# A two-layer conv, latent-attention and expert step on one core: expert matrices with eight rows per partition, and a reordered further round

## The reference, cut to what matters

```python
for e in range(N_EXPERTS):                       # 16
    h = jax.nn.silu(t @ w1[e]) * (t @ w3[e])     # w1, w3: 1024 x 512
    out = out + gates[:, e:e + 1] * (h @ w2[e])  # w2: 512 x 1024
```

## Time and profile before

| what | us |
|---|---|
| median of 3 runs | 1077.71 |
| lowest, highest of them | 1077.51, 1089.82 |
| profiled execution, its own time | 1089.26 |
| span of its trace | 1087.6 |
| layer 0's experts, on PE (from about 207 to 476) | 269 |
| layer 1's experts, on PE (from about 794 to 1071) | 277 |

### The profile page before, as it was taken

One profiled execution on the slowest core, in us unless ns is written; L12 is line 12 of the kernel. 1 busy time (PEld: TensorE's weight loads), 2 busy tenths in 40 slices (PEclk: granted clock), 3 DMA queues, 4 the chain that ended last, 5 costly groups with the idle time before them and its releaser, 6 DMA issues.

```text
span 1087.6 us, 14379 instructions
## 1 busy us (share of the span) xinstructions
PE 964.6 (89%) x4814; PEld 480.5 (44%) x4815; DVE 339.5 (31%) x815; ACT 168.6 (16%) x335; POOL 105.5 (10%) x198
## 2 busy tenths in 40 slices
PE   6979989899989989979989888889798999888993
PEld 4646535443333333336646644454543333332331
DVE  0935464522122221251234432304522122211125
ACT  1000042111111110012123232220111111011100
POOL 0260000101000000013000033000110000000000
PEclk9989999799999999989998899989698999999997
DMA  7974454999979999977213101566386499999981
GB/s 188 253 242 126 126 195 154 345 370 329 379 264 362 377 375 385 395 243 251 59 35 101 64 20 53 199 222 262 127 286 239 169 370 376 378 383 378 383 306 49
DMA packets 131654, 266.96 MB, mean 245 GB/s; under 512 B 7480, under 2 KB 39252, under 8 KB 131585
## 3 DMA queue, kind: packets, MB, share of 16 engines
q1 hardware_dynamic: 121200, 237.74, 61.9%
q10 hardware_dynamic: 5009, 16.15, 4.2%
q0 software_dynamic: 5392, 12.34, 4.1%
HBM read 259.78 MB, written 7.15 MB: 245 GB/s over the span
## 4 chain that ended last, share of the span: by engine, by line
PE 71%; DMA 8%; DVE 8%; SPq 8%; ACT 4%; issue 2%; DVEq 0%; ACTq 0%
PE bank L1009 16%; PE bank L1017 9%; DMA w<-in_e_w 5%; PE wide L1052 4%; PE bank L902 4%; SPq L420 4%; PE bank L791 3%; PE bank L956 3%; DMA dbuf<-in_a_w_pw 3%; SPq L423 3%; PE wide L902 3%; PE wide L791 2%; PE wide L1809 2%; PE bank L807 2%; PE bank L1787 2%
## 5 line engine op out<-in xcount | busy, mean ns | idle before, releaser
L1009 PE MATMUL bank<-w,dbuf 128*64 128x512 f32 x960 | 216.5, 604 | 16.3 <-DMA w<-in_e_w 14.6
L1009 PEld LDWEIGHTS bank<-w,dbuf 128*64 128x64 f32 x960 | 74.2, 139 | 153.9 <-issue 153.6
L1017 PE MATMUL bank<-w,dbuf 128*64 128x512 f32 x480 | 122.6, 657 | 10.9 <-DVE dbuf L1455 10.9
L1460 DVE COPY dbuf<-bank 64x512 f32<-64x512 f32 x64 | 44.1, 689 | 166.3 <-PE bank L1017 165.8
L1451 DVE TENSOR_TENSOR dbuf<-dbuf,bank 64x512 f32<-64x512 f32 x32 | 22.1, 690 | 201.6 <-ACT dbuf L709 201.6
L709 ACT ACTIVATE dbuf<-bank 64x512 f32<-64x512 f32 x32 | 18.9, 592 | 412.8 <-PE bank L1009 412.8
L1017 PEld LDWEIGHTS bank<-w,dbuf 128*64 128x64 f32 x480 | 40.4, 149 | 77.7 <-issue 77.7
L1052 PE MATMUL wide<-dbuf,ukT 128*128 128x512 f32 x128 | 62.9, 617 | 3.0 <-DVE dbuf L1460 3.0
L549 POOL COPY idx_col<-idx 64x1 int32 (+1 forms) x32 | 5.8, 180 | 560.8 <-PE bank L956 375.8
L956 PEld LDWEIGHTS bank<-ident,dbuf 64*128 64x128 f32 x448 | 38.9, 160 | 41.4 <-issue 36.8
L536 POOL DMA_DIRECT2D w<-in_cache_kpe x64 | 34.4, 538 | 217.3 <-PE bank L1787 116.7
(11 more groups left out here) (365 smaller groups left out, 1148.1 us busy)
## 6 DMA issues: line engine op xcount, KB each, us to landing
w<-in_e_w SPq DMA_DIRECT2D x90, 2048.0 KB
dbuf<-in_a_w_pw SPq DMA_DIRECT2D x16, 512.0 KB, 7.3
w<-u_rows SPq DMA_DIRECT2D x32, 142.0 KB, 3.0
dbuf<-in_a_w_pw ACTq DMA_DIRECT2D x1, 4096.0 KB, 17.1
dbuf<-in_e_w SPq DMA_DIRECT2D x2, 2048.0 KB, 14.9
w<-in_cache_ckv SPq DMA_DIRECT2D x32, 128.0 KB, 2.8
dbuf<-in_cache_ckv SPq DMA_DIRECT2D x32, 128.0 KB, 2.1
dbuf<-in_b_w_o SPq DMA_DIRECT2D x2, 2048.0 KB, 8.6
```

Source lines behind the costliest of these rows:

```text
L1009: last = nc.tensor.matmul(bank[n * C:(n + 1) * C], x[:, k], w[n][k], start=(k == 0), stop=(k == KD - 1))
L1017: last = nc.tensor.matmul(bank[n * C:(n + 1) * C], h[:, k], w[k][:, n * 512:(n + 1) * 512], start=(k == 0), stop=(k == 3))
L1460: last = V.tensor_copy(y_pair[s * C:(s + 1) * C, h * 512:(h + 1) * 512], DOWN[h * C:(h + 1) * C, :])
```

## The change

Four edits. The rows of the first and third matrices are split as "(p k)", so a partition gets rows 8p to 8p + 7, 16 KB that adjoin in DRAM and in SBUF. Channel 8p + k then has to be at partition p of block k of the turned tokens, so `turn_rows` (for gathered rows) and `turn_more` read every eighth element of the gathered row; the hidden rows turn as before. In the further round PE waits for `y_copied` only ahead of the down product, and turns `hot_more` behind a new semaphore `m_built`, ahead of the hidden rows; `up_more` takes the eight blocks in another order in each quarter. The semaphore `own_ready` is gone, `own` counts on `ld_att`.

```diff
-                src = a[("e_w1", "e_w3")[n]][l].rearrange("e (k p) f -> p e k f", p=P)[:, bass.ds(e, 1)]
+                src = a[("e_w1", "e_w3")[n]][l].rearrange("e (p k) f -> p e k f", p=P)[:, bass.ds(e, 1)]
...
-            def turn_rows(bank, src, n, r0=0):
+            def turn_rows(bank, src, n, r0=0, strided=True):
+                cols = src.rearrange("c (p k) -> c k p", k=n) if strided else src.rearrange("c (k p) -> c k p", k=n)
                 for k in range(n):
-                    last = nc.tensor.matmul(bank[:, k * C:(k + 1) * C], src[:, k * P:(k + 1) * P],
+                    last = nc.tensor.matmul(bank[:, k * C:(k + 1) * C], cols[:, k],
                                             ident[r0:r0 + C, r0:r0 + C], start=True, stop=True, is_transpose=k > 0)
...
             def turn_more():
+                cols = xg_more.rearrange("c (p k) -> c k p", k=KD)
                 for k in range(KD):
-                    last = nc.tensor.matmul(TURN[:, k * H:(k + 1) * H], xg_more[:, k * P:(k + 1) * P], ident[0:H, 0:H],
+                    last = nc.tensor.matmul(TURN[:, k * H:(k + 1) * H], cols[:, k], ident[0:H, 0:H],
...
             def up_more(w):
-                for k in range(KD):
+                for at in range(KD):
                     for q in range(4):
-                        n, lo = q // 2, q % 2 * (FE // 2)
+                        n, lo, k = q // 2, q % 2 * (FE // 2), (at + 2 * q) % KD
                         last = nc.tensor.matmul(UP[q * H:(q + 1) * H, 0:FE // 2], xe_more[:, k],
-                                                w[n][k][:, lo:lo + FE // 2], start=(k == 0), stop=(k == KD - 1))
+                                                w[n][k][:, lo:lo + FE // 2], start=(at == 0), stop=(at == KD - 1))
...
-                turn_rows(UP, hid, 4).then_inc(ht_turned, 1)
+                turn_rows(UP, hid, 4, strided=False).then_inc(ht_turned, 1)
...
                         pe.wait_ge(xe_copied, g0 + E if isinstance(e, int) and e == E - 1 else e + (g0 + 2))
-                        pe.wait_ge(y_copied, e + (g0 + 1))
                         pe.wait_ge(m_xg, (first + c) * 16)
                         turn_more().then_inc(m_turned, 1)
                         pe.wait_ge(m_copied, first + c)
                         up_more(W13[w]).then_inc(m_up, 1)
-                        pe.wait_ge(m_hid, first + c)
-                        turn_hidden_more().then_inc(m_ht, 1)
+                        pe.wait_ge(m_built, first + c)
                         for i, (t0, m) in enumerate(TILES):
                             last = nc.tensor.transpose(TURN[:, t0:t0 + m], hot_more[0:m, i].rearrange("p q c -> p (q c)"),
                                                        ident[0:m, 0:m])
                         last.then_inc(m_hot, 1)
+                        pe.wait_ge(m_hid, first + c)
+                        turn_hidden_more().then_inc(m_ht, 1)
                         pe.wait_ge(m_htc, first + c)
+                        pe.wait_ge(y_copied, e + (g0 + 1))
                         down_more(W2[w]).then_inc(m_down, 1)
...
             def build_more(c, e):
                 for i in range(3):
...
+                last.then_inc(m_built, 1)
...
-            act.dma_start(own, a["c_own"]).then_inc(own_ready, 16)
+            act.dma_start(own, a["c_own"]).then_inc(ld_att, 16)
...
-            dve.wait_ge(own_ready, 16)
+            dve.wait_ge(ld_att, 80)
```

More of the change, by code:

```diff
@@ L331, in trunk_step @@
                              "down_done", "y_copied"))
+        m_built = sem("more_built")
         m_idx, m_xg, m_hot, m_hotc, m_turned, m_copied, m_up, m_act, m_hid, m_ht, m_htc, m_down, m_y = (
@@ L352, in trunk_step @@
         cpe_ready = [sem("cpe_ready0"), sem("cpe_ready1")]
-        ols_ready, ols_turned, ols_copied, uv_done, oT_copied, own_ready = (
-            sem(n) for n in ("ols_ready", "ols_turned", "ols_copied", "uv_done", "oT_copied", "own_ready"))
+        ols_ready, ols_turned, ols_copied, uv_done, oT_copied = (
+            sem(n) for n in ("ols_ready", "ols_turned", "ols_copied", "uv_done", "oT_copied"))
         ext_s = ext[:, :, EXTP:EXTP + DB * EXTS].rearrange("p k (b s) -> p k b s", b=DB)
@@ L1431, in build_more @@
                 for i in range(3):
-                    V.tensor_scalar(hot_more[:, i],
-                                    route[:, bass.ds(c * H + (R_IOTA + 1 + H), H)].unsqueeze(1).to_broadcast([P, 4, H]),
-                                    rank1[:, i, bass.ds(e, 1)], gates[:, i, bass.ds(e, 1)], ALU.is_equal, ALU.mult)
+                    last = V.tensor_scalar(hot_more[:, i], route[:, bass.ds(c * H + (R_IOTA + 1 + H), H)].unsqueeze(1)
+                                           .to_broadcast([P, 4, H]), rank1[:, i, bass.ds(e, 1)],
+                                           gates[:, i, bass.ds(e, 1)], ALU.is_equal, ALU.mult)
+                last.then_inc(m_built, 1)
             def build_pair(e, n):
```

## The result

The changed kernel takes 1076.3 us (median of 20 runs, 1070.67 to 1082.98); the kernel before, run between them on the same chip, 1084.05 (20 runs, 1077.51 to 1090.28). The ratio is 0.9928, 95% interval 0.9907 to 0.9948: 7.8 us less. The forecast was 15.9 us less.

The account below looks back on a forecast made before the run. TensorE was taken as the bound, with a DMA-bound inset. Terms -11.6 - 4.6 - 3.3 - 1.4 + 4.0 + 1.0 = -15.9 us took the profiled 1089.3 to 1073.4, the median 1077.7 to 1062; 80% range 1050 to 1082.

Parts of the forecast that it names:

- Waits for matrices, 14.6 to 3 left: TensorE's waits for expert matrices in both layers shrink from 14.6 us to 3 as weights come sooner: gain 11.6 us.
- Strided turn, +4: Weight loads of the 32 turns read 32 bytes apart; a quarter of a doubling (15.4 us) taken, +4 us.
- Slow products behind the two longest waits, -4.6: Up products behind the two longest matrix waits, ahead of expert 12, no longer run slow: 4.6 us saved.
- The round, -3.3 and -1.4: Two further rounds: no wait for VectorE's output copy, 3.3 us; half the slow layer 1 up product's excess, 1.4 us.
- First gather, +1.0: Layer 0's first gather, without slack, lands later behind the large pieces: 1.0 us lost.
- Rate and period: Weight DMAs: 16 KB pieces estimated at 432 GB/s; period per expert falls from 17.15 to 16.0 to 16.5 us.
- A: Rival, chance 0.30: the stride doubles the turns' loads, 15.4 us instead of 4, no DMA wait left; 7.5 us less, 1070.
- B: Rival, chance 0.09: the stride makes each turn's nine loads four times as long, 46 us; 1101 us, slower than before.
- C: Rival, chance 0.09: the weight DMA rate does not rise and the waits stay; only the round gains, 1076 us.
- D: Rival, chance 0.10: gathers starve behind large pieces and each of 16 turns waits, 27 us at 13 us landing; 1089.

Follow-up runs that it names:

- permuted store: The changed kernel, but GpSimd stores x's rows already in block order, so turns read adjoining elements from 16 KB pieces: 1068.0 us, 0.9868 of before.
- the round alone: The kernel before plus only the further-round and semaphore edits, with layout and turn as before: 1080.5 us, 0.995 of before.
- second matrix: The kernel with the permuted store, plus second matrix in 16 KB pieces and VectorE writing the gated product in permuted order: 1073.0 us, 0.9861 of before.
- two rows: The changed kernel with two adjoining rows per partition instead of eight (4 KB pieces, turn reads 8 bytes apart): 1077.5 us, 0.9915 of before.
- small pieces: The changed kernel with first and third matrices landing in 2 KB pieces again, strided turn kept: 1089.3 us, 1.0044 of before.
- 8 KB permuted: The kernel with the permuted store, but four adjoining rows per partition (8 KB pieces): 1066.9 us, 0.9836 of before.
- the layout alone: The changed kernel's eight-row layout and strided turn, with the further round waiting and ordering products as before: 1079.3 us, 0.9975 of before.
- four rows: The changed kernel with four adjoining rows per partition instead of eight (8 KB pieces, turn reads 16 bytes apart): 1072.9 us, 0.9889 of before.

## Why the prediction was wrong

The direction held, and 1076.3 lies in the range of 1050 to 1082; the gain was half of the forecast. (The forecast stood on a median of three runs, 1077.7; on the 1084.05 of twenty it would have said 1068.) By its own steps:

1. **Waits for matrices, 14.6 to 3 left: the number came out, the working didn't.** Measured 2.9 over the span. But the step assumed a turn that costs next to nothing, and with such a turn 12.3 us are left (the kernel with the permuted store), at the very period that the step had worked out. What fails is that expert 12 "hangs on the eight pairs of loads" and gains their whole saving: what PE itself gains on the way is given back in front of the matrix. After has 2.9 because its turns are late and its pieces large: the same late turns with 2 KB pieces have 11.7. How much of the 12.3 goes back to the edits and how much to a quicker execution (the down products of that trace are 10.2 us shorter than before's) no run parts.
2. **Strided turn, +4: the step that failed.** "I take a quarter of the doubling" should have been the whole: 0.57 us a turn against the doubling of 0.48, 18.2 us on the loads, of which 1.4 are hidden again. Behind the first turns of the two layers come 3.2 us of slower up products; the 1.7 of them in layer 1 go with the stride in all ten traces. VectorE's strided read, the row it leaned on, said nothing about PE, and it set a sum of groups of four beside a maximum over 128, two different reductions; the argument that spoke for the doubling (PE does a load of 128 elements and a product in 81 ns, VectorE takes 243 for as many elements, 1.9 ns each and not about one) stood in the text and was given a quarter.
3. **Slow products behind the two longest waits, -4.6: came in this trace.** After has no wait over 1.35 us ahead of an up product, and the products that took 8.78 and 9.99 take 7.09. The group of up products is only 1.6 us shorter (216.5 to 214.9), because 3.2 came back at the first ones of the layers. The sentence behind it, that waits of such a size carry no slow product, does not hold in general: of the six waits of 2.2 to 2.7 us in the ten traces three were followed by a product of 8.55 to 8.78 us, while one of 3.29 us with the permuted store was followed by one of 7.09.
4. **The round, -3.3 and -1.4: right.** 5.1 and 5.4 us by two pairs of kernels, against 4.7, which is within their intervals. Of the clock's part half of 2.8 was taken; in every kernel with the new order layer 1's product runs in 3.66 (3.83 with columns in pairs), so in the traces all 2.8 came. The copy and the hidden rows changed places at no cost, as forecast (0.52 more ahead of L990, 0.6 less ahead of L982). The turned order of the blocks showed no cost: both products take 3.66, as layer 0's did before.
5. **First gather, +1.0:** -0.4 in this trace. What the large pieces delayed was the store of x (16.0 us), which no step named.
6. **Rate and period: right.** 438 GB/s for matrices alone, 416 to 438 in shorter stretches (432 estimated), 16.1 to 16.6 us per expert where PE is fast enough to show it (16.0 to 16.5).

**The rivals.** A is what happened: it said 7.5 us less, 7.8 were measured, and the mechanism (a load with about its 128 columns once more: 0.57 us a turn, 0.48 said) is the measured one. Part of that closeness is luck: it let all 14.6 us of waits go and put 15.4 on the turns, where 11.7 and 17.6 were seen, and it had nothing of the 3.2 at the first up products. B is out (1.30 us, not 2), C is out (438 GB/s), D is out: gathers in after land after 3.7 to 11.3 us, median 7.7, and PE waits for none behind the first.

**The clock.** Before and after have these two groups of down products:

```profile
L1017 PE MATMUL bank<-w,dbuf 128*64 128x512 f32 x480 | 122.6, 657 | 10.9 <-DVE dbuf L1455 10.9
```
```profile
L1020 PE MATMUL bank<-w,dbuf 128*64 128x512 f32 x480 | 113.9, 617 | 10.9 <-DVE dbuf L1460 10.9
```

8.7 us apart, with the same 480 products. Over the ten traces this group goes with the mean granted clock: 122.6 at 0.935 (before), 119.1 at 0.938 (the round alone), 120.0 and 117.2 at 0.940 (second matrix, two rows), 113.7 at 0.942 (small pieces), 120.9 at 0.943 (8 KB permuted), 110.6 at 0.947 (the layout alone), 113.9 and 112.4 at 0.950 (after, permuted store), 110.5 at 0.953 (four rows). In part that is one thing seen twice, since products at 1.2 GHz are what lowers the mean. The executions of one kernel differ in the same way: after took 1070.7 us at 0.950 and 1083.0 at 0.940.

So 10.5 of the 18.3 us between the two traces belong to their executions (5.2 and 5.4 us off the medians of their runs), and a forecast that takes slow products from one trace as the kernel's own can count a saving that no edit brings. Whether the 8.7 us are that or the change's stays open: the five kernels with a strided turn have 110.5 to 117.2 us in this group, the five without 112.4 to 122.6, and no kernel was traced twice. Whether the change raises the mean clock a little (the median of its runs is 0.946, of before 0.938 to 0.943 by chip) stays open as well: no run separates it from the shorter waits.

## What to carry to other kernels

A layout that makes a transfer contiguous moves the stride to whoever reads it next; price that reader by its own rate, and look for a place where the reorder is paid once (here the store of x ahead of all gathers) instead of once per use. When two engines alternate in being late, terms don't add: take the saving of one with the other's time held, then once more with it changed; a wait that shrinks is no proof that the transfers got faster. And a slow product is a property of the kernel only if it is slow in more than one trace, as layer 1's first up product was with every strided turn.

## What the runs showed of the hardware

- TensorE's weight loads from float32 with gaps: nine of them in 0.73 us with adjoining elements, 1.13 at 8 bytes, 1.36 at 16, 1.30 at 32, whatever the size of the DMA pieces.
- Layer 1's first up product behind a turn of 1.30 us in place of 0.73, and the same 0.78 us of waiting: 8.78 us against 7.09, at a granted clock of 0.81 against 1.00 (8.78 in five kernels, 7.09 in five).
- VectorE's product over 64 x 512 with each output element 512 bytes from the one before, in groups of four: 1050 ns against 690. GpSimd's copy of 1024 elements per partition, read 32 bytes apart, took 2.04 us.
- Over the same 130 us with everything in flight, pieces of 2 KB gave 378 and 379 GB/s, of 4 KB 393, of 8 KB 397 and 398, of 16 KB 391 to 399; 16 KB pieces alone 438 over 7 us, 2 KB pieces alone 388 over 9.
- A store of 64 rows on ACT's queue beside 16 KB pieces landed after 16.0 us, in the kernel with the layout alone after 16.3; with 8 KB pieces the slowest of these stores took 10.5, with 2 KB pieces 7.2 and 7.5.
